# Streaming every gemm pass of a two-layer block from its last column to its first

## What is computed

```python
proj = u @ w_in[l]                                       # block 1: mixer input, 1024 -> 6152
mix = jnp.concatenate([h, y], axis=-1) @ w_out[l]        # 2048 -> 1024
up = causal_dwconv(u @ ffn_up[l], ffn_conv_w[l], ffn_conv_b[l])
f = (jax.nn.silu(gt) * a) @ ffn_down[l]                  # 2816 -> 1024
proj = jnp.einsum('bsd,de->bse', h, w_in)                # blocks 2 and 3: attention, then a gated recurrence
gate, up = jnp.split(jnp.einsum('bsd,df->bsf', h, w_in), 2, axis=-1)
return jnp.einsum('bsf,fd->bsd', jax.nn.silu(gate) * up, w_out)
```

## Time and profile before

| | us |
|---|---|
| median of 2 timed runs | 2200.8 (2200.31 to 2201.29) |
| the profiled execution, its device time | 2200.2 |
| the same execution, span from first to last instruction | 2198.1 |
| mean granted TensorE clock over the span | 0.994 of full speed |

### The profile page before, as it was taken

One profiled execution on the slowest core, in us unless ns is written; L12 is line 12 of the kernel. 1 busy time (PEld: TensorE's weight loads), 2 busy tenths in 40 slices (PEclk: granted clock), 3 DMA queues, 4 the chain that ended last, 5 costly groups with the idle time before them and its releaser, 6 DMA issues.

```text
span 2198.1 us, 26833 instructions
## 1 busy us (share of the span) xinstructions
PE 2138.4 (97%) x9588; PEld 1709.5 (78%) x9588; DVE 1117.0 (51%) x1982; ACT 663.2 (30%) x1142; POOL 1498.2 (68%) x741
## 2 busy tenths in 40 slices
PE   7999999999999999999999999999999999999997
PEld 3878777768888887788868888886788777888886
DVE  6899974884444103777643222105877835222101
ACT  3413335123222103444442111104555534111100
POOL 5868575667777887644379777886333348877785
PEclk9999999999999999999999999999999999999999
DMA  6323223732333332222123333332222222333332
GB/s 247 107 84 96 77 78 106 268 142 96 95 95 96 105 105 86 80 84 78 48 76 106 96 97 99 102 106 83 59 67 68 68 68 77 96 96 98 102 105 86
DMA packets 56371, 215.98 MB, mean 98 GB/s; under 512 B 6216, under 2 KB 6216, under 8 KB 53088
## 3 DMA queue, kind: packets, MB, share of 16 engines
q1 hardware_dynamic: 52992, 206.96, 29.3%
q10 hardware_dynamic: 3296, 7.91, 1.1%
HBM read 212.70 MB, written 2.15 MB: 98 GB/s over the span
## 4 chain that ended last, share of the span: by engine, by line
PE 78%; DVE 10%; POOL 4%; ACT 3%; issue 3%; DMA 2%; SPq 0%; DVEq 0%; POOLq 0%; ACTq 0%
PE ps L371 63%; DVE y L2036 3%; PE ps L603 2%; PE ps L1192 2%; DMA raw<-in_wstream 2%; PE ps L408 2%; POOL w_hi L974 1%; POOL w_lo L980 1%; PE ps L1284 1%; PE ps L1130 1%; PE ps L1315 1%; PE ps L1421 1%; PE ps L1302 1%; ACT u_hi L476 1%; DVE u_lo L526 1%
## 5 line engine op out<-in xcount | busy, mean ns | idle before, releaser
L980 POOL TENSOR_TENSOR w_lo<-raw,w_hi 128x1024 fp32r<-128x1024 f32 x335 | 813.6, 2429 | 199.3 <-ACT w_hi L1879 175.5
L974 POOL TENSOR_TENSOR w_hi<-raw,ones 128x1024 fp32r<-128x1024 f32 x304 | 582.9, 1918 | 368.9 <-DMA raw<-in_wstream 368.3
L371 PE MATMUL ps<-u_hi,w_hi 128*128 128x512 f32 x1760 | 708.9, 403 | 7.1 <-DVE qk L2047 2.8
L371 PE MATMUL ps<-u_hi,w_lo 128*128 128x512 f32 x1760 | 687.9, 391 | 0.0
L371 PE MATMUL ps<-u_lo,w_hi 128*128 128x512 f32 x1760 | 686.5, 390 | 0.0
L371 PEld LDWEIGHTS ps<-u_hi,w_hi 128*128 128x128 f32 x1760 | 332.1, 189 | 77.2 <-issue 6.7
L371 PEld LDWEIGHTS ps<-u_hi,w_lo 128*128 128x128 f32 x1760 | 331.1, 188 | 71.2
L371 PEld LDWEIGHTS ps<-u_lo,w_hi 128*128 128x128 f32 x1760 | 331.9, 189 | 66.9 <-issue 3.6
L371 PE MATMUL ps<-f_hi,w_lo 128*128 128x512 f32 x528 | 205.4, 389 | 0.0
L371 PE MATMUL ps<-f_hi,w_hi 128*128 128x512 f32 x528 | 205.4, 389 | 0.0
L371 PE MATMUL ps<-f_lo,w_hi 128*128 128x512 f32 x528 | 205.4, 389 | 0.0
(11 more groups left out here) (366 smaller groups left out, 2901.4 us busy)
## 6 DMA issues: line engine op xcount, KB each, us to landing
raw<-in_wstream SPq DMA_DIRECT2D x342, 512.0 KB, 3.6
ada_buf<-in_ada SPq DMA_DIRECT2D x16, 1024.0 KB, 7.3
ada_start<-in_ada SPq DMA_DIRECT2D x8, 1024.0 KB, 17.0
cbc<-decay_rows ACTq DMA_DIRECT2D x7, 512.0 KB, 3.5
x<-in_xT SPq DMA_DIRECT2D x1, 2048.0 KB, 8.0
bc<-gate_rows ACTq DMA_DIRECT2D x4, 512.0 KB, 5.3
out_T<-x ACTq DMA_DIRECT2D x8, 256.0 KB, 2.2
prm<-in_params SPq DMA_DIRECT2D x1, 357.5 KB, 2.9
```

The lines of the kernel that those rows point to most:

```text
L371: last = nc.tensor.matmul(out, a, b, start=(start and k == 0 and i == 0), stop=(stop and k == nk - 1 and i == 2))
L974: g.tensor_tensor(w_hi[slot][:], raw[slot][:], ones[:, 0:1].to_broadcast([P, D]), ALU.mult).then_inc(chunk_hi, 1)
L980: g.tensor_tensor(w_lo[slot][:], raw[slot][:], w_hi[slot][:].bitcast(f32), ALU.subtract).then_inc(chunk_split, 1)
```

## The change

A helper `back(t)` returns the view `t[:, ::-1]`. Every gemm pass takes its moving operand and its output through it, so both access patterns start at column 511 and have a step of minus one element. Column j of the product still goes to column j of the bank. Stationary operands, the chains, `start` and `stop`, all waits, increments, DMAs and every other engine's instructions stay as they are; no instruction is added, removed or moved on any engine. The diff, cut where it repeats:

```diff
+    def back(t):
+        return t[:, ::-1]
+
     def gemm_chunk(pe, chunk, slot, out, hi, lo, k0, nk, start, stop, tile_wait=None, hook=None):
...
-            for i, (a, b) in enumerate(tri(wh, wl, hi(k), lo(k))):
-                last = nc.tensor.matmul(out, a, b, start=(start and k == 0 and i == 0),
+            for i, (a, b) in enumerate(tri(wh, wl, back(hi(k)), back(lo(k)))):
+                last = nc.tensor.matmul(back(out), a, b, start=(start and k == 0 and i == 0),
                                         stop=(stop and k == nk - 1 and i == 2))
...
-                nc.tensor.matmul(outs_[g], wh, u_tiles(k), start=(k == 0), stop=False)
-                nc.tensor.matmul(outs_[g], wl, u_tiles(k), start=False, stop=False)
+                nc.tensor.matmul(back(outs_[g]), wh, back(u_tiles(k)), start=(k == 0), stop=False)
+                nc.tensor.matmul(back(outs_[g]), wl, back(u_tiles(k)), start=False, stop=False)
             tile_wait(k)
             for g, (wh, wl) in enumerate(weights):
-                last = nc.tensor.matmul(outs_[g], wh, u_lows(k), start=False, stop=(k == KT - 1))
+                last = nc.tensor.matmul(back(outs_[g]), wh, back(u_lows(k)), start=False, stop=(k == KT - 1))
...
```

More of the change, by code:

```diff
@@ L406, in step @@
             wh, wl = w_hi[slot][:, k * P:(k + 1) * P], w_lo[slot][:, k * P:(k + 1) * P]
-            for i, (a, b) in enumerate(tri(wh, wl, u_tiles(k), u_lows(k))):
-                last = nc.tensor.matmul(outs_[g], a, b, start=(k == 0 and i == 0), stop=(k == KT - 1 and i == 2))
+            for i, (a, b) in enumerate(tri(wh, wl, back(u_tiles(k)), back(u_lows(k)))):
+                last = nc.tensor.matmul(back(outs_[g]), a, b, start=(k == 0 and i == 0), stop=(k == KT - 1 and i == 2))
             if k == KT - 1:
@@ L601, in step @@
             wh, wl = w_hi[slot][:, k * P:(k + 1) * P], w_lo[slot][:, k * P:(k + 1) * P]
-            for i, (a, b) in enumerate(tri(wh, wl, self.hi(k), self.lo(k))):
-                last = nc.tensor.matmul(self.out(n), a, b, start=(k == 0 and i == 0), stop=(k == KT - 1 and i == 2))
+            for i, (a, b) in enumerate(tri(wh, wl, back(self.hi(k)), back(self.lo(k)))):
+                last = nc.tensor.matmul(back(self.out(n)), a, b, start=(k == 0 and i == 0), stop=(k == KT - 1 and i == 2))
             return last
@@ L631, in finish @@
             for n, (wh, wl) in enumerate(weights):
-                nc.tensor.matmul(self.out(n), wh, self.hi(k), start=False, stop=False)
-                nc.tensor.matmul(self.out(n), wl, self.hi(k), start=False, stop=False)
+                nc.tensor.matmul(back(self.out(n)), wh, back(self.hi(k)), start=False, stop=False)
+                nc.tensor.matmul(back(self.out(n)), wl, back(self.hi(k)), start=False, stop=False)
             pe.wait_ge(self.ready.sem, self.ready.at("lo", k))
             for n, (wh, wl) in enumerate(weights):
-                last = nc.tensor.matmul(self.out(n), wh, self.lo(k), start=False, stop=True)
+                last = nc.tensor.matmul(back(self.out(n)), wh, back(self.lo(k)), start=False, stop=True)
                 if n or not self.kept:
@@ L1190, in wout_pe @@
                 wh, wl = w_hi[c % SLOTS][:, k * P:(k + 1) * P], w_lo[c % SLOTS][:, k * P:(k + 1) * P]
-                for i, (a, b) in enumerate(tri(wh, wl, hi[:, k, :], lo[:, k, :])):
-                    last = nc.tensor.matmul(ps[n % GROUP][:], a, b, start=(half == first and k == 0 and i == 0),
+                for i, (a, b) in enumerate(tri(wh, wl, back(hi[:, k, :]), back(lo[:, k, :]))):
+                    last = nc.tensor.matmul(back(ps[n % GROUP][:]), a, b, start=(half == first and k == 0 and i == 0),
                                             stop=(half != first and k == KT - 1 and i == 2))
```

## The result

The changed kernel takes 2235.7 us (2234.7 to 2236.7, two runs) against 2200.8 us: 1.0159 times as long, with a 95% interval of 1.0115 to 1.0202. It is slower by about 35 us. The prediction said 2200.5 us with no change within 2%, and 0.08 for a fixed price per pass that comes to more than 2%. The move is inside 2% but clearly more than nothing.

A forecast was written before the change was run, and what follows sets the result against it. The prediction took TensorE's gemm passes, limited by column rate, to bound the kernel. 2200.2 us plus 8064 passes at 0 ns gave 2200.2 us for the profiled execution, 2200.5 us as the forecast; range 2190 to 3930 us.

The forecast's parts named there:

- a fixed price per pass: Rival: each gemm pass pays at its start, full rate inside; 2310 us if the 13.6 ns doubled; chance 0.08 above 2%.
- The bound: TensorE's gemm passes at L371 limit the kernel by column rate, 226.9 ns each, about 1830 of 2198.1 us.
- Nothing hides them: Claim that the gemm passes all lie exposed, since TensorE's waits are small, the largest 13.8 us.
- The write: Descending write of each pass into its PSUM bank, priced together with the read at 0 ns per pass.
- half rate: Rival: read or write path pairs columns only ascending, two clocks a column; 3780 to 3920 us, chance 0.28.
- the likeliest case: No change within 2%, chance 0.57, with a range of its own of 2190 to 2225 us.
- The read: Descending moving read from SBUF in each pass, put at 0 ns from DVE's backward writes and TensorE's jump at L1389.
- The 13.6 ns: What each 226.9 ns pass adds to 213.3 ns of streaming, said to have nothing to do with direction.
- The count: 8064 gemm passes in the whole kernel, 2688 tiles by three, each taken at 0.2269 us.
- Each ns per pass is 8.06 us: Scale from a price per gemm pass to kernel time; 44 us, or 2%, needs 5.5 ns.
- The term for what is hidden: Time a slower stream would win back as the weight supply runs ahead, 0 to 60 us over the kernel.
- The Trainium skill's rules: PSUM: non-contiguous patterns slow matmuls significantly; SBUF: at least two accesses in a row should hit one 16-byte line.

The follow-up runs named there:

- e3: The changed kernel with only the bank written descending and the moving operand read ascending: 2198.4 us, ratio 0.9995.
- e1: The kernel before plus rows of 21 gemm-like passes per access pattern after the last gemm: 512 columns take 226.7 ns ascending, 233.5 descending.
- e2: The changed kernel with only the moving operand read descending and the bank written ascending: 2235.5 us, ratio 1.0158.
- e11: The kernel before plus rows of 42 passes whose moving read starts at other columns, up or down: ascending 226.7 to 238.2 ns, descending 233.3 to 235.5.
- e10: The changed kernel with only the 3312 gemm passes outside the feed-forward parts descending: 2205.7 us, ratio 1.0031.
- e7: The changed kernel with groups of four columns in order, descending inside each, on both sides: 2199.7 us, ratio 1.0001.
- e6: The changed kernel with groups of four columns from last to first, ascending inside each, on both sides: 2235.7 us, ratio 1.0169.
- e8: The kernel before plus rows of 42 passes with other weight widths, weight places or tiles: ascending 226.7 to 233.7 ns, descending 233.3 or 233.4.
- e5: The kernel before plus rows of 42 passes with the moving read reversed by group size or width: 512 columns 226.7 ns ascending, 233.4 descending.

## Why the prediction was wrong

**The bound.** Right in the feed-forward parts: there the passes of L371 set the time, and the whole change shows in the distance between two of them. "Nothing hides them" was wrong for the rest. In block 1's mixer DVE holds the path for long stretches (its 10% of the chain stood in the earlier trace rows), and passes that grew by 8.9 us made it 4.3 us longer.

**The write.** Right: 0 ns (e3), and half rate, the heavy rival with 0.28, did not come on either side. It was priced far too likely, and with it the range, up to 3930 us, far too wide: 2235.7 us lies in it, but so would have nearly anything. That the time fell into the range is owed to the half-rate rival, which had nothing to do with it; the range of the likeliest case, 2190 to 2225 us, was missed.

**The read.** Wrong, and this is the step that failed: "I take the lower end, 0", on the ground that "neither a backward step nor a jump has any price in the trace". The row for the jump, L1389 against L1413, is plain fp32, at two clocks a column. e1 shows that plain fp32 has no price even for a full reversal (429.2 and 429.1 ns), so this row could not have shown one. The other row was DVE's writes, another engine and the other direction of traffic. The pass under question takes one clock a column, and neither row runs at that rate. What the runs show in place of the 0 is 6.6 ns for each pass of a long row, all of it from the read (e2, e3); why the read costs it stays open.

**The 13.6 ns.** Wrong in the same place: "the 13.6 ns around it have nothing to do with direction". They are no constant of the pass. They were 13.6 in the good case, become 20.2 when the order of lines runs down, and vary from 13.4 to 24.9 ns for ascending reads with the column they start at (e11: 226.7 to 238.2 ns). The rival of a fixed price named their doubling; the measured growth, half of them, lies just above the 5.5 ns that I had set as the point where 2% is reached, and the time rose by 1.6% only because the count was wrong too.

**The count.** "Each ns per pass is 8.06 us" was wrong by a third. 6.6 ns gave 35 us and not 53. The two steps that failed here are that each pass stood in a stream at 226.9 ns and that nothing hid it. Of the 3312 passes outside the feed-forward parts many stand behind other matmuls and waits, where the ascending pass had not reached its best, and of the growth of the others a part fell into TensorE's idle time; e10 leaves 1.8 ns each. The term for what is hidden was in the prediction, 0 to 60 us for a half-rate pass, but not in "each ns per pass". The trace had the other reason: the chain's pieces of nine passes in the attention were 2.13 us, 237 ns a pass with the entry, against 226.9 in the pure stretches. (The count itself, 8064, is right. The row of L398 in the earlier trace rows is the (w_hi, lo) pass and not the (w_hi, hi) one; their numbers are equal.)

**The Trainium skill's rules.** Neither rule that I weighed decided the case: the write has no price, and the read's isn't that of two columns in a line, as e7 (neighbours reversed, free) and e6 (neighbours kept, full price) show.

## What to carry to other kernels

A row that is to bound a price must run at the same speed as the operation under question: slack in a slower form hides exactly the few ns that are asked for. Where a stream of equal matmuls is the bound, read the distance between starts, and ask of its share beyond one column per clock what it hangs on; here some 3% hang on the order in which the columns are read, on the column at which the moving tile starts, and on the place of the weights. Multiply a price per instruction only by the instructions that stand where it was measured, and only in the stages in which the chain runs through them.

## What the runs showed of the hardware

- A 512-column fp32r pass has two usual lengths in a stream, 226.7 and 233.4 ns, 16 clocks of 2.4 GHz apart. The first was lost with fewer weight columns (230.1 with 64, 231.5 with 32), with weights moved by 4, 16 or 32 columns (233.7, 233.5 and 232.5, the stream still ascending, e8), and with a read that descends all through (233.4). It was kept, to 226.7 in the last ten passes of a row, with weights moved by 64 columns, with weights and moving tile moved together by 16 or 32 (by 4 it was lost, 233.2), with the read reversed inside groups of four, and with blocks of 64 columns or more from last to first.
- Behind other work an ascending pass reaches 226.7 ns only after some passes: 226, 236, 228, 233, 230, 227 in the row from column 64 (e11).
- An ascending read from column 1 costs 238.2 ns, from columns 0, 64 and 128 226.7 to 227.1 (e11).
- Groups of 16 columns in order but descending inside cost 266.5 to 266.7 ns, with 32 weight columns as with 128 (e5, e8). Why is open.
- Every second column in an fp32r read halves its rate (256 columns, 230 ns against 120); every second column in a plain fp32 write to PSUM costs nothing (215.8 ns both, at two clocks a column).
- The order in which a PSUM bank is filled had no price where it alone was changed (e3: 2198.4 us against 2199.0; the row of e1 is at 226.7 ns in its last ten passes).
